# The retention's key rotation moved from VectorE to GpSimd in a two-block float32 kernel

## What is computed

```python
h = rms_norm(x, attn_norm_w)
proj = h @ w_in                       # r_q, r_k, r_v, r_g (512 each), c_q 256, c_kv 128, k_pe 32
q = rope(r_q.reshape(B, S, 8, 64), positions)
k = rope(r_k.reshape(B, S, 8, 64), positions) * 64 ** -0.5
o = retention(q, k, v)                # q k^T with a decay mask, times v; then group norm and silu gate
# latent attention: q from c_q @ w_uq (8 heads of 64 + 32), k and v from c_kv @ w_ukv,
# the last 32 of each query head and k_pe rotated too; softmax
x = x + concat(y_ret, y_mla) @ w_out
x = x + conv_ffn(rms_norm(x), w_up, ..., w_down)

def rope(x):  # x1, x2: halves of the last dimension; cos, sin by position
    return concat(x1 * cos - x2 * sin, x1 * sin + x2 * cos)
```

## Time and profile before

| | |
|---|---|
| median of 3 runs | 864.73 us (864.62 to 867.03) |
| the profiled execution, its own time | 865.75 us |
| its span, first to last instruction | 863.8 us |
| mean granted clock of TensorE | 0.988 |
| TensorE matmuls busy | 832.2 us, 96% |
| VectorE / ScalarE / GpSimd busy | 564.1 (65%) / 459.9 (53%) / 45.9 us (5%) |
| loads | 141.58 MB, mean 164 GB/s |

### The profile page before, as it was taken

One profiled execution on the slowest core, in us unless ns is written; L12 is line 12 of the kernel. 1 busy time (PEld: TensorE's weight loads), 2 busy tenths in 40 slices (PEclk: granted clock), 3 DMA queues, 4 the chain that ended last, 5 costly groups with the idle time before them and its releaser, 6 DMA issues.

```text
span 863.8 us, 13295 instructions
## 1 busy us (share of the span) xinstructions
PE 832.2 (96%) x5226; PEld 743.5 (86%) x5226; DVE 564.1 (65%) x856; ACT 459.9 (53%) x669; POOL 45.9 (5%) x100
## 2 busy tenths in 40 slices
PE   6999897999999998999999999999999999999997
PEld 5887786999999996888888888888998899999996
DVE  5895556676667667647888873577667555555553
ACT  6663644654555546566556655555754444444441
POOL 0000100000000000000423230010000000000000
PEclk9999798999999999999999999999999999999999
DMA  9664112455555564656454545143256365655551
GB/s 335 238 195 146 50 49 97 154 190 194 193 187 177 194 222 145 193 179 195 146 173 136 180 151 189 51 126 119 99 170 205 115 200 189 194 177 179 182 192 49
DMA packets 89740, 141.58 MB, mean 164 GB/s; under 512 B 3664, under 2 KB 56272, under 8 KB 89568
## 3 DMA queue, kind: packets, MB, share of 16 engines
q1 hardware_dynamic: 89552, 140.84, 49.5%
q10 hardware_dynamic: 144, 0.13, 0.1%
HBM read 139.91 MB, written 1.05 MB: 163 GB/s over the span
## 4 chain that ended last, share of the span: by engine, by line
PE 90%; DVE 4%; ACT 4%; issue 1%; DMA 1%; SPq 0%; DVEq 0%; ACTq 0%
PE bank L458 27%; PE bank L459 26%; PE bank L460 26%; PE bank L342 3%; PE bank L787 2%; ACT w_hi L974 2%; DVE w_lo L1340 1%; PE bank L877 1%; PE bank L847 1%; DMA raw<-in_w_in 1%; PE bank L607 1%; PE bank L807 0%; ACT arena L985 0%; ACT arena L1257 0%; DVE h_lo L1374 0%
## 5 line engine op out<-in xcount | busy, mean ns | idle before, releaser
L1340 DVE TENSOR_TENSOR w_lo<-raw,w_hi 128x1024 fp32r<-128x1024 f32 (+2 forms) x260 | 306.8, 1205 | 103.1 <-ACT w_hi L974 102.2
L974 ACT CAST w_hi<-raw 128x1024 fp32r<-128x1024 f32 (+2 forms) x260 | 263.1, 1035 | 151.9 <-PE bank L460 145.8
L458 PE MATMUL bank<-h_hi,w_hi 128*128 128x256 f32 x744 | 214.5, 288 | 2.7 <-DVE h_lo L1374 2.7
L460 PE MATMUL bank<-h_hi,w_lo 128*128 128x256 f32 x744 | 211.1, 284 | 0.0
L459 PE MATMUL bank<-h_lo,w_hi 128*128 128x256 f32 x744 | 211.1, 284 | 0.0
L458 PE MATMUL bank<-w_hi,h_hi 128*128 128x512 f32 (+1 forms) x352 | 140.0, 398 | 10.1 <-DVE w_lo L1340 8.7
L458 PEld LDWEIGHTS bank<-h_hi,w_hi 128*128 128x128 f32 x744 | 142.4, 191 | 7.6 <-issue 5.9
L459 PEld LDWEIGHTS bank<-h_lo,w_hi 128*128 128x128 f32 x744 | 142.5, 191 | 1.2
L460 PEld LDWEIGHTS bank<-h_hi,w_lo 128*128 128x128 f32 x744 | 142.4, 191 | 0.2
L460 PE MATMUL bank<-w_hi,h_lo 128*128 128x512 f32 (+1 forms) x352 | 137.6, 391 | 0.0
L459 PE MATMUL bank<-w_lo,h_hi 128*128 128x512 f32 (+1 forms) x352 | 137.5, 391 | 0.0
(11 more groups left out here) (201 smaller groups left out, 883.7 us busy)
## 6 DMA issues: line engine op xcount, KB each, us to landing
raw<-in_w_in SPq DMA_DIRECT2D x46, 1024.0 KB, 5.1
raw<-in_w_up SPq DMA_DIRECT2D x22, 1024.0 KB, 5.0
raw<-in_w_ff_up SPq DMA_DIRECT2D x16, 1024.0 KB, 5.4
raw<-in_w_ff_down SPq DMA_DIRECT2D x16, 1024.0 KB, 4.9
raw<-in_w_down SPq DMA_DIRECT2D x11, 1024.0 KB, 4.9
raw<-in_w_out SPq DMA_DIRECT2D x8, 1024.0 KB, 5.0
raw<-in_w_gla_branch SPq DMA_DIRECT2D x4, 1024.0 KB, 5.0
raw<-in_w_attn_branch SPq DMA_DIRECT2D x2, 1024.0 KB, 5.0
```

The lines of the kernel that those rows point to most:

```text
L458: nc.tensor.matmul(dst, l_hi, r_hi, start=start, stop=False)
L460: return nc.tensor.matmul(dst, l_lo, r_hi, start=False, stop=stop)
L974: nc.scalar.copy(dst, raw_half(m % RAW, half, size, cols)).then_inc(s.hi_done, 1)
L1340: nc.vector.tensor_tensor(dst, raw_half(n // 2 % RAW, n % 2, size, cols), h, ALU.subtract).then_inc(s.lo_done, 1)
```

## The change

GpSimd rotates the retention's keys, both tiles, at the head of its program, with temporaries of its own (`rope_tmp_k`, words 512 to 1023 of the arena, between `rope_tmp` and the rest). It waits for `trig` and for `acc_free0` 2 and raises the new `ret_k_roped`, for which TensorE waits in place of `ret_roped` 2. VectorE's two key rotations go. `lo(18)` moves behind the latent queries' tile 0, in front of `lo(19)`.

```diff
-    "ret_roped ret_q_turned ...
+    "ret_roped ret_k_roped ret_q_turned ...
...
         rope_tmp = area(0, 2, RH * RD // 2)
+        rope_tmp_k = area(512, 2, RH * RD // 2)
...
+            ret_k = proj[:, :, 512:1024].rearrange("p a (h c) -> p a h c", c=RD)
+            half = RD // 2
+            t1, t2 = [rope_tmp_k[:, f, :].rearrange("p (h f) -> p h f", f=half) for f in range(2)]
+            gp.wait_ge(s.trig, 1)
+            gp.wait_ge(s.acc_free0, 2)
+            for a in range(TT):
+                x1, x2 = ret_k[:, a, :, 0:half], ret_k[:, a, :, half:RD]
+                cos, sin = [angle[:, f, a, 0:half].rearrange("p (o f) -> p o f", o=1).to_broadcast([P, RH, half])
+                            for f in range(2)]
+                nc.gpsimd.tensor_tensor(t1, x1, sin, ALU.mult)
+                nc.gpsimd.tensor_tensor(t2, x2, sin, ALU.mult)
+                nc.gpsimd.tensor_tensor(x1, x1, cos, ALU.mult)
+                link(nc.gpsimd.tensor_tensor(x2, x2, cos, ALU.mult))
+                nc.gpsimd.tensor_tensor(x1, x1, t2, ALU.subtract)
+                ins = nc.gpsimd.tensor_tensor(x2, x2, t1, ALU.add)
+                if a == 0:
+                    link(ins)
+            ins.then_inc(s.ret_k_roped, 1)
+
             for n in range(2 * AG + 2):
...
             chunk_rows(16, 7, 512, h, halves=(2,))
-            pe.wait_ge(s.ret_roped, 2)
+            pe.wait_ge(s.ret_k_roped, 1)
             turn_tiles(4, lambda a, k: proj[:, a, 512 + k * P:640 + k * P], s.ret_k_turned, (6, 7))
...
             link(rotate(ret_q, RH, RD, 0, 0))
             lo(15, 16)
             rotate(ret_q, RH, RD, 0, 1).then_inc(s.ret_roped, 1)
             lo(17)
-            dve.wait_ge(s.ret_roped, 1)
-            dve.wait_ge(s.acc_free0, 2)
-            link(rotate(ret_k, RH, RD, 0, 0))
-            lo(18)
-            rotate(ret_k, RH, RD, 0, 1).then_inc(s.ret_roped, 1)
 
             dve.wait_ge(s.acc_free1, 2)
             dve.wait_ge(s.acc_free0, 3)
-            dve.wait_ge(s.ret_roped, 2)
+            dve.wait_ge(s.ret_roped, 1)
             link(rotate(q_tok[:, :, :, NOPE:QK], MH, PE_D, 32, 0))
-            lo(19)
+            lo(18, 19)
             rotate(q_tok[:, :, :, NOPE:QK], MH, PE_D, 32, 1).then_inc(s.mla_q_ready, 1)
```

More of the change, by code:

```diff
@@ L194 @@
     "mla_turned mla_pt mla_pv mla_o "
-    "ret_roped ret_q_turned ret_k_turned ret_qT ret_kT ret_scores ret_masked ret_o_head ret_copied "
+    "ret_roped ret_k_roped ret_q_turned ret_k_turned ret_qT ret_kT ret_scores ret_masked ret_o_head ret_copied "
     "ret_centred ret_sq ret_y mixed_turned mixed_hi mixed_lo "
@@ L1457, in _ @@
             lo(14)
-            ret_q, ret_k = [proj[:, :, c:c + 512].rearrange("p a (h c) -> p a h c", c=RD) for c in (0, 512)]
+            ret_q = proj[:, :, 0:512].rearrange("p a (h c) -> p a h c", c=RD)
             dve.wait_ge(s.acc_free1, 1)
```

## The result

The kernel after takes 872.06 us (median of 5 runs, 871.0 to 873.85) against 866.06 us (median of 5, 864.62 to 867.03) for the kernel before: ratio 1.0071, interval 1.0054 to 1.0087, some 6 us slower. (The median before was 864.73 us over the three runs that the prediction starts from.) The profiled execution took 873.85 us, the slowest of the five, with a span of 872.1.

What follows compares the result with a forecast made beforehand. TensorE was taken as the bound, waiting where VectorE's halves come late. Twelve delays of 0.58 us, less 0.73 slack and 0.29 recovered wait, gave +5.9 us on 864.73: 870.6 us, range 864.3 to 873.5.

Steps and rivals of the forecast that it cites:

- The bound: TensorE, busy 96%, bounds the kernel; VectorE's work from 40 to 75 us counts only where TensorE waits for it.
- at most 0.3 us: The most to be won from removing VectorE's key rotations: TensorE's wait for w_lo between 40 and 75 us.
- The 0.29 us in brackets: TensorE's wait at 59.73 for lo(19), which ended at 59.68; forecast to go.
- The exclusion: GpSimd and VectorE instructions reading two SBUF operands exclude each other; each GpSimd instruction of 256 elements delays VectorE by 0.58 us.
- GpSimd's 1.17 and 4.57 us: Lengths at 447.23 and 461.10 of small GpSimd instructions beside VectorE's two-operand ones; undisturbed 0.22 us.
- Its other direction: That VectorE also waits for GpSimd, for the time of GpSimd's data: 0.58 us per instruction of 256 elements.
- a start-to-start difference of 0.03 us: VectorE's lines 1716 and 1717 start 1.14 us apart without a GpSimd service between, 1.17 with one of 16 elements.
- The turns: One GpSimd instruction after each VectorE instruction from 44.5 to 50.1 us: 12 x 0.58 = 6.96 us before lo(17).
- one for every second instruction: Variant within the forecast's 0.62: GpSimd misses each second short rotation instruction, 7 turns before lo(17), +4.4 us, 869.1.
- The clock: A long TensorE pause at half 17 may lower the granted clock: up to 2 us more, not a separate case.
- The rival of starvation: VectorE's runs never break, GpSimd's keys come after 58.41 us: +5 to +10 us, middle about 873; chance 0.15.
- The rival without delay: GpSimd waits but VectorE does not, before lo(17): 864.4 us; chance 0.23, with delays below 0.3 us per instruction.

Runs made afterwards that it cites:

- no_rotation: The kernel after without GpSimd's key rotation; one 128x16 memset raises the semaphore, keys stay unrotated. Ratio 0.9998; half 12 to the scores 30.02 us, -0.59.
- added_only: The kernel before, VectorE keeping its key rotations, plus 12 GpSimd products of 128x256 on scratch words. Ratio 1.0083; half 12 to the scores +6.06 us.
- size512: The kernel before plus 6 GpSimd products of 128x512 on scratch words. One run, no ratio; half 12 to the scores 36.84 us, +6.23.
- vector_delay: The kernel before plus 8 VectorE products of 128x480, 3 ahead of lo(15, 16), 5 ahead of lo(17), GpSimd idle there. Ratio 1.0064, stretch +6.00 us.
- late_start: The kernel after, but GpSimd begins its key rotation only when lo(17) is done. Ratio 1.0048; half 12 to the scores +3.55 us.
- half_dose: The kernel after with only tile 0 of the keys on GpSimd, tile 1 rotated by VectorE. Ratio 1.0035; half 12 to the scores +1.93 us.
- lo17_early: The kernel after with VectorE's order changed: lo(15, 16, 17), the queries' tile 1, then lo(18). Ratio 1.0023; half 12 to the scores +2.54 us.

## Why the prediction was right

The way, the place and the size held: 870.6 was forecast, +5.9 us, and +6.0 was measured. Its parts did not all hold, and the close number is in part luck.

- *The bound.* TensorE waited only where VectorE's halves were late. Right, but "at most 0.3 us" to be won was too small: no_rotation wins 0.59 us up to the scores, which the whole time does not show. The 0.29 us in brackets left out the 0.24 by which the half would have begun ahead of the transposes' modelled end.
- *The exclusion, read from GpSimd's 1.17 and 4.57 us.* Right. Its other direction, which rested on a start-to-start difference of 0.03 us, was right too: 0.54 us a turn measured. I took 0.58, from 2.25 ns an element; it is 2.1. VectorE's own side gave 0.48.
- *The turns.* One for one, as forecast, and not one for every second instruction. But 11 fell before the end of `lo(17)`, not 12: GpSimd's first instruction, 1.46 us long, got in only behind VectorE's fourth product, and its last was served behind `lo(17)`. They cost 0.51 us each on average, as two of them fell on the pauses that a rotation's `link` makes and cost 0.41 and 0.43. This term was too large: 6.96 us forecast for `lo(17)`, 5.6 measured. TensorE's half 17 was late by 4.9 us, not 6.2, and its waits for `w_lo` were 4.0 us, not about 6.
- *The clock.* I kept it out of the sum, as "an addition to the forecast in its upper range", "up to 2 us more". It came: 1.7 us. The step that failed is to leave at nothing what stands behind a pause "of some 4 us"; 3.81 us of pause were enough, as were 3.84 in added_only, 4.01 in size512 and 3.50 in vector_delay. The 3.0 us of late_start and the 1.3 of half_dose and lo17_early left it at 1.00. Yet the length of the pause alone does not decide: elsewhere in the kernel the same wait of 1.47 us left the clock at 1.00 in one execution and at 0.57 in another, as the result's rows show, and behind a wait of 2.00 us it was 0.63 over 4 us in before (from 678.20) and 1.00 in after (from 687.82). So half_dose's expectation, that a pause of 2 us or less does not lower the clock, held there and is no rule.
- *What comes back.* 0.29 us forecast, 0.5 measured, for the reason given under the bound.

So 4.9 + 1.7 - 0.5 = 6.1 stands for 6.2 - 0.3 = 5.9. The turns were 1.3 us too large and the clock 1.7 too small, and these errors nearly cancelled: that is luck. The rival of starvation did not happen (GpSimd's longest instruction took 1.70 us), though late_start shows that its wait is real once GpSimd starts later. The rival without delay falls with added_only; its threshold of 0.09 us a turn is far from 0.54.

## What to carry to other kernels

Before work goes to an idle GpSimd, look at what VectorE reads at that time. If VectorE reads two SBUF operands, or runs a fast copy SBUF to SBUF (128x512 in 0.42 us), the two engines share one budget. Each element of a two-operand GpSimd product then takes 2.1 ns from VectorE, while VectorE's own 0.34 us for 256 elements is 1.3 ns an element, so the move costs VectorE more than it takes off. What left VectorE alone here was GpSimd products beside copies from PSUM, and memsets. The few small GpSimd instructions of a trace can tell this ahead: look for one that ends 0.07 us behind a VectorE instruction.

And put the clock into the price of a new pause of TensorE: behind the four of 3.5 to 4.0 us made here it cost 1.7 to 2.3 us. Shorter ones are not safe either: behind waits of 1.47 and 2.00 us elsewhere in this kernel it fell in some executions and not in others.

## What the runs showed of the hardware

- A GpSimd product with a constant (128x256, one tensor) takes 0.85 us alone, longer than one of two tensors, 0.72; it holds VectorE off for 0.2 us in place of 0.54.
- Twelve GpSimd memsets of 128x1024, 1.01 us each, left all of VectorE's two-operand instructions at 0.42 us.
- VectorE is held off for the data and not for the whole GpSimd instruction: 0.27, 0.54 and 1.11 us for 128, 256 and 512 elements, where 256 take 0.72 us alone.
- A GpSimd product that started beside a copy of VectorE's from PSUM took 2.72 us, held until the `lo` that VectorE ran next was over.
- Behind pauses of TensorE of 3.5 to 4.0 us its matmuls of 128x512 took 0.63 us each for 3 to 4.5 us, at the lower clock. In the changed stretch pauses of 3.0 us and less left it at 1.00; elsewhere the same wait of 1.47 us was followed by 1.00 in before and by 0.57 in after.
